# A mixer's output projection between the last steps of its recurrence, with reordered scaled products and a halved inverse level

## The reference, cut to what matters

```python
def wkv_scan(S0, r, w, k, v, kk, bb, reverse):
    def step(S, inp):
        rt, wt, kt, vt, kkt, bt = inp
        sk = jnp.einsum('bhij,bhj->bhi', S, kkt)
        S = S * wt[:, :, None, :] - sk[..., None] * bt[:, :, None, :] + vt[..., None] * kt[:, :, None, :]
        return S, jnp.einsum('bhij,bhj->bhi', S, rt)
    ...
# even_mixer, behind the two scans of each direction
o_lat = rwkv_output(ys_l[0] + ys_l[1], r_l, (dirs_l[0][1], dirs_l[1][1]), v_l, g_l, r_k, gn_w, gn_b)
out_lat = jnp.concatenate([o_lat, f_lat], axis=-1) @ w_out        # [256, 1024] @ [1024, 1024]
# the block, behind the mixer
h_lat = h_lat + m_lat[5] * o_lat
h_lat = half_ffn(h_lat, m_lat, 6, norm_g[i, 2], ffn2_w_gu[i], ffn2_w_down[i])   # rmsnorm, gate, up, silu, down
```

## Time and profile before

| | |
|---|---|
| median of three runs | 3303.49 us |
| the profiled execution | 3305.29 us |
| its span, first to last instruction | 3303.5 us |
| PE busy | 3195.9 us (97%), 28282 instructions |
| DVE busy | 2169.4 us (66%), 4656 instructions |
| ACT busy | 542.0 us (16%), 1073 instructions |
| GpSimd busy | 172.2 us (5%), 200 instructions |
| mean granted clock of PE | 0.989 |

### The profile page before, as it was taken

How to read it: one execution, slowest core, us unless ns; L and a number is a source line. 1 busy time by engine, 2 the same in 40 slices (tenths; PEclk the granted TensorE clock), 3 DMA queues, 4 the chain that set the end, 5 groups by cost and what they waited for, 6 DMA issues and landing times.

```text
span 3303.5 us, 64967 instructions
## 1 busy us (share of the span) xinstructions
PE 3195.9 (97%) x28282; PEld 2874.2 (87%) x28282; DVE 2169.4 (66%) x4656; ACT 542.0 (16%) x1073; POOL 172.2 (5%) x200
## 2 busy tenths in 40 slices
PE   7999999899999899999999999999999999999998
PEld 4888445588888799999889999999999999999998
DVE  6886347666676377676647657676667576776675
ACT  2000010234433110110121011122110102120111
POOL 1000000122222000000000000000000000000000
PEclk9999999999999899999999999999999999999999
DMA  7455555100000144444334465333444443334343
GB/s 287 178 220 220 223 211 221 44 6 6 7 6 7 51 160 173 154 171 174 131 129 171 173 209 183 117 127 136 162 158 175 147 160 116 128 122 166 136 171 115
DMA packets 69230, 466.48 MB, mean 141 GB/s; under 512 B 7296, under 2 KB 9984, under 8 KB 16217
## 3 DMA queue, kind: packets, MB, share of 16 engines
q1 hardware_dynamic: 51696, 368.07, 31.2%
q0 software_dynamic: 12192, 87.04, 7.0%
q10 hardware_dynamic: 5065, 7.27, 0.7%
HBM read 456.59 MB, written 5.77 MB: 140 GB/s over the span
## 4 chain that ended last, share of the span: by engine, by line
PE 91%; DVE 6%; ACT 2%; issue 1%; DMA 0%; POOL 0%; ACTq 0%; DVEq 0%; POOLq 0%
PE ps L776 31%; PE ps L1229 18%; PE ps L831 8%; PE ps L671 8%; PE ps L1380 4%; PE ps L855 4%; PE ps L906 1%; PE ps L893 1%; PE ps L912 1%; PE ps L1248 1%; PE ps L1303 1%; PE ps L1174 1%; PE ps L1278 1%; PE ps L953 1%; PE ps L1006 1%; PE ps L1355 1%
## 5 line engine op out<-in xcount | busy, mean ns | idle before, releaser
L776 PE MATMUL ps<-arena 128*128 128x128 f32 x4400 | 519.1, 275 | 0.0
L776 PEld LDWEIGHTS ps<-arena 128*128 128x128 f32 x4400 | 505.0, 192 | 0.0
L776 PE MATMUL ps<-arena,ring 128*128 128x128 f32 x2200 | 275.0, 275 | 0.0
L1825 DVE TENSOR_TENSOR arena<-arena,ps 128x256 f32<-128x256 f32 x146 | 61.5, 421 | 311.2 <-ACT arena L1431 285.3
L776 PEld LDWEIGHTS ps<-arena,ring 128*128 128x128 f32 x2200 | 260.9, 192 | 0.5
L1950 DVE CUSTOM_DVE_ANT_0 arena<-arena,vec 128x1024 f32<-128x1024 f32 x168 | 206.6, 1280 | 1.7 <-DMA arena<-in_ada_t 1.7
L1229 PE MATMUL ps<-y,arena 128*128 128x128 f32 x1584 | 193.3, 276 | 0.6 <-DVE y L2439 0.6
L1229 PEld LDWEIGHTS ps<-y,arena 128*128 128x128 f32 x1584 | 184.6, 192 | 4.8 <-issue 3.4
L1790 DVE TENSOR_TENSOR arena<-ring 128x512 f32<-128x512 f32 (+1 forms) x170 | 113.9, 670 | 60.0 <-DMA ring<-in_w_f_down 32.5
L671 PE MATMUL ps<-arena,ring 128*128 128x512 f32 x352 | 152.2, 592 | 0.0
L671 PEld LDWEIGHTS ps<-arena,ring 128*128 128x128 f32 x352 | 66.9, 190 | 83.8 <-issue 83.7
(11 more groups left out here) (393 smaller groups left out, 5871.5 us busy)
## 6 DMA issues: line engine op xcount, KB each, us to landing
ring<-in_w_f_gu SPq DMA_DIRECT2D x88, 1024.0 KB, 4.8
arena<-in_ada_t POOLq DMA_DIRECT2D x72, 1024.0 KB, 5.2
ring<-in_w_fx_gu SPq DMA_DIRECT2D x44, 1024.0 KB, 4.8
ring<-in_w_f_down SPq DMA_DIRECT2D x36, 1024.0 KB, 4.8
ring<-in_w_fx_down SPq DMA_DIRECT2D x24, 1024.0 KB, 4.8
ring<-in_w_qk_a SPq DMA_DIRECT2D x18, 1024.0 KB, 4.8
ring<-in_w_qk_r SPq DMA_DIRECT2D x16, 1024.0 KB, 4.8
ring<-in_w_v_r SPq DMA_DIRECT2D x16, 1024.0 KB, 4.8
```

The source lines that it names most:

```text
L776: last = mm(out, weights[number][:, j * P:(j + 1) * P], inputs[number](base + j), start=(s.opens and j == 0 and number in (1, 5)), stop=(s ...
```

## The change

The projection's weights are cut by input tile instead of output tile (`rows` in place of `cols`; `EVEN_ORDER` puts the two Fourier tiles first). Its 64 products run input tile by input tile into eight accumulating output tiles in banks 0, 1, 3 and 4: 40 of them behind the steps of period 12, 16 behind steps 1, 3 and 6 of period 13, and 8, those of tile 5, at the end. DVE takes each pair of output tiles out as it is complete; the norm's sums move to bank 5 and stand behind all products. Of the first two weight sums of `f2_0`, one moves to the end of period 12 and one behind the last update. In `scaled`, `bt` and `kt_` come before `kr`, PE waits for each by itself, `key_of` of an even unit moves from step 8 to step 5, and the operation L2196 moves from `key_scales` into `key_of`. Of level 5 only the half of `tri` that `halves_x` reads is computed; its transpose stays whole.

```diff
 STREAM += _ffn("f1_0", "ffn1_w_gu", DFF, "ffn1_w_down", 0)
-STREAM += [("e_in", 11, 1, "cols", "e_w_in", 0, 0), ("e_out", 4, 1, "cols", "e_w_out", 0, 0)]
+STREAM += [("e_in", 11, 1, "cols", "e_w_in", 0, 0), ("e_out", 4, 1, "rows", "e_w_out", 0, 0)]
+EVEN_ORDER = (6, 7, 0, 1, 2, 3, 4, 5)
 STREAM += _seven("f2_0", "ffn2_w_gu", DFF, "ffn2_w_down", 0) + _seven("f1_1", "ffn1_w_gu", DFF, "ffn1_w_down", 1)
...
+        def even_tile(m):
+            return ps[:, (0, 1, 3, 4)[m // 2], m % 2 * SEQ:(m % 2 + 1) * SEQ]
+        def norm_bank(name):
+            return 5 if name == "n2" else 4
         def norm_sums(t):
...
                     for k in range(tiles * g, tiles * g + tiles):
-                        last = mm(seg2(4)[:, 0:segs], ones[:], sq[:, :, k], start=(k == 0), stop=(k == KD - 1))
+                        last = mm(seg2(norm_bank(name))[:, 0:segs], ones[:], sq[:, :, k], start=(k == 0), stop=(k == KD - 1))
                     if g == groups - 1:
...
                     for c in range(4):
-                        for rows in (FIRST, SECOND):
+                        for rows in (sides(u)[:1] if lev == LEVELS - 1 else (FIRST, SECOND)):
                             last = mm(ps[rows, 0, at(hd, c)], tri_t[rows, q, hd, c], x_sb[rows, hd, c],
...
             def keys_tok(u):
-                pe.wait_ge(*past(f"dve.kt{u}"))
+                pe.wait_ge(*past(f"dve.bt{u}"))
                 if u % 2 == 0:
...
                     pe.wait_ge(*past(f"dve.bon_v{u // 2}"))
+                pe.wait_ge(*past(f"dve.kt{u}"))
                 for c in range(4):
...
                 pe.wait_ge(*past(f"act.g{u // 2}"))
+                pe.wait_ge(*past(f"dve.kr{u}"))
                 if u % 2:
...
+            even_slots, even_made = list(slots_flat("e_out")), [0]
+            def even_products(count):
+                for i in range(even_made[0], even_made[0] + count):
+                    n, m = divmod(i, KD)
+                    k, s = EVEN_ORDER[n], even_slots[n // 2]
+                    if i == 0:
+                        pe.wait_ge(*past(f"act.x{UNITS - 1}_{LEVELS}"))
+                        pe.wait_ge(*past(f"dve.t_off{UNITS - 1}"))
+                        pe.wait_ge(*past(f"dve.k_mix{UNITS - 1}"))
+                    if i % 16 == 0:
+                        pe.wait_ge(landed[s.pos], landed_by("e_out", s))
+                    if m == 0 and k < KR:
+                        pe.wait_ge(*past(f"dve.mixed{k}"))
+                    w = ring[:, s.pos, (n % 2 * KD + m) * P:(n % 2 * KD + m + 1) * P]
+                    last = mm(even_tile(m), w, y1(k), start=(n == 0 and m % 2 == 0), stop=(n == KD - 1), skip_group_check=True)
+                    if i % 16 == 15:
+                        last.then_inc(slots_used, 1)
+                    elif n == KD - 1 and m % 2:
+                        last.then_inc(*step(f"pe.even{m // 2}"))
+                even_made[0] += count
+            BESIDE_CHUNKS = (0, 0, 4, 4, 4, 4, 4, 4, 4, 3, 3, 3, 3)
+            BESIDE_READOUT = {1: 3, 3: 3, 6: 10}
+            def beside(p, n):
+                if p == UNITS:
+                    even_products(BESIDE_CHUNKS[n])
+                elif p == UNITS + 1:
+                    even_products(BESIDE_READOUT.get(n, 0))
             for p in range(-1, UNITS + 2):
...
                     between(p, 2 * lev - 1)
+                    beside(p, 2 * lev - 1)
                     if unit(p):
...
                     between(p, 2 * lev)
+                    beside(p, 2 * lev)
                 if unit(p):
...
                 between(p, 2 * LEVELS - 1)
+                beside(p, 2 * LEVELS - 1)
                 if unit(p):
...
                 between(p, 2 * LEVELS)
-            pe.wait_ge(*past(f"dve.mixed{KR - 1}"))
-            linear("e_out", y1, SEQ, behind=sums_behind("n2"))
+                beside(p, 2 * LEVELS)
+            even_products(KD)
+            norm_sums_of = sums_behind("n2")
+            for g in range(4):
+                norm_sums_of(g)
             seven("f2_0", y1, "n2", sums_behind("n3"))
...
                 act.wait_ge(*past(f"pe.{name}_sum"))
-                f(rs[:, 0:segs], seg2(4)[:, 0:segs], ACT.Sqrt, bias=V("eps6"), scale=1.0 / D) \
+                f(rs[:, 0:segs], seg2(norm_bank(name))[:, 0:segs], ACT.Sqrt, bias=V("eps6"), scale=1.0 / D) \
                     .then_inc(*step(f"act.{name}_std"))
...
-            def first_weight_sums(name):
-                for s, stage in seven_slots(name)[0:2]:
+            def first_weight_sums(name, which=slice(0, 2)):
+                for s, stage in seven_slots(name)[which]:
                     weight_sums(s, stage)
...
                         continue
-                    if s.item == 3:
+                    if s.item == 3 and name != "e_out":
                         first_weight_sums(after_third)
-                    v.wait_ge(slots_used, s.n + 1)
+                    if name == "e_out" and s.item < 3:
+                        v.wait_ge(*past(f"pe.even{s.item}"))
+                    else:
+                        v.wait_ge(slots_used, s.n + 1)
                     for m in range(tiles):
...
                             assert segs == 1
-                            last = stt(hv, tile_of(s, m),
+                            last = stt(hv, even_tile(k) if name == "e_out" else tile_of(s, m),
                                        gate_f[:, bass.ds(at + 2 * k + sgm, 1)], hv, ALU.mult, ALU.add)
                     last.then_inc(psum_free, 1)
+                    if s.item == 3 and name == "e_out":
+                        first_weight_sums(after_third, slice(1, 2))
...
                 v.wait_ge(*past(f"pe.t{u}_{lev}"))
-                tt(eight(tri[:, q]), eight(tri[:, q]), four_eight(0), ALU.subtract).then_inc(*step(f"dve.t{u}_{lev}"))
+                rows = sides(u)[0] if lev == LEVELS - 1 else slice(0, P)
+                tt(eight(tri[rows, q]), eight(tri[rows, q]), four_eight(0)[rows], ALU.subtract) \
+                    .then_inc(*step(f"dve.t{u}_{lev}"))
                 v.wait_ge(*past(f"pe.tt{u}_{lev}"))
...
                     v.wait_ge(*past(f"pe.k_mix{u - 1}"))
-                ts(kd, rate[:, d], V("k_a", t), omka[:, t:t + 1], ALU.mult, ALU.add).then_inc(*step(f"dve.kd_a{u}"))
                 tt(bb, kk, rate[:, d], ALU.mult).then_inc(*step(f"dve.bb{u}"))
...
                 d, t = u % 2, u // 2
+                v.wait_ge(*past(f"act.sig{t}"))
+                ts(kd, rate[:, d], V("k_a", t), omka[:, t:t + 1], ALU.mult, ALU.add).then_inc(*step(f"dve.kd_a{u}"))
                 v.wait_ge(*past(f"dve.kd_a{u}"))
...
                 v.wait_ge(*past(f"act.exp{u}"))
+                v.wait_ge(*past(f"dve.bb{u}"))
+                tt(bt, bb, p_inv_f, ALU.mult).then_inc(*step(f"dve.bt{u}"))
+                tt(kt_, kd, p_inv_f, ALU.mult).then_inc(*step(f"dve.kt{u}"))
                 tt(kr[:, g, 0:4], kk.rearrange("p (c t) -> p c t", c=4), ex, ALU.mult)
-                tt(kr[:, g, 4:6], r_of(u // 2).rearrange("p (c t) -> p c t", c=2), own[:, 0:2], ALU.mult)
-                tt(bt, bb, p_inv_f, ALU.mult)
-                tt(kt_, kd, p_inv_f, ALU.mult).then_inc(*step(f"dve.kt{u}"))
+                tt(kr[:, g, 4:6], r_of(u // 2).rearrange("p (c t) -> p c t", c=2), own[:, 0:2], ALU.mult) \
+                    .then_inc(*step(f"dve.kr{u}"))
                 for j in range(3):
...
                         key_inverse(u // 2, n)
+                    elif n == 5:
+                        key_of(u)
                     elif n == 7:
...
                     elif n == 8:
-                        key_of(u)
                         scaled(u)
...
                 fill(p, 12)
+                if p == UNITS:
+                    first_weight_sums("f2_0", slice(0, 1))
             v.wait_ge(*past(f"dve.mixed{KR - 1}"))
...
             laid = laid[list(E_IN_PAIRS)] if name == "e_in" else laid
+        elif cut == "rows":
+            laid = w[list(EVEN_ORDER)].reshape(n_slots, 2, P, KD, P).transpose(0, 2, 1, 3, 4)
         elif cut == "pair":
```

More of the change, by code:

```diff
@@ L86 @@
            "w_in_2", "w_attn_proj_2", "w_ret_proj_2", "w_out_2", "w_ffn_gate_2", "w_ffn_up_2", "w_ffn_down_2")
-SLOT_USED = {"cols": SLOT, "pair": SLOT, "down": DOWN_SLOT, "tall": SLOT, "flat": 3 * 512, "quarters": SLOT, "quarters_cols": SLOT,
+SLOT_USED = {"cols": SLOT, "rows": SLOT, "pair": SLOT, "down": DOWN_SLOT, "tall": SLOT, "flat": 3 * 512, "quarters": SLOT, "quarters_cols": SLOT,
              "quarters_tall": SLOT, "quarters_pairs": SLOT,
```

## The result

The changed kernel takes 3271.69 us (median of four runs, 3270.77 to 3272.80) against 3304.68 us (four runs, 3298.15 to 3306.09): 33.0 us less, a ratio of 0.9901 with a 95% interval of 0.9887 to 0.9915. I had forecast 3283.7 us, 3276 to 3293: right in direction, 13 us short in size, outside my range. The profiled execution took 3271.81 us with a span of 3270.0 us, 33.5 us less than the one before.

What follows compares the result with a forecast made beforehand. TensorE was taken as the bound (91% of the chain of waits). Terms 15.6 (tail) - 0.6 (halved level) + 3.1 (scaled products) + 1.7 (clock) = 19.8 us took the median from 3303.5 to 3283.7 us, range 3276 to 3293.

Steps and rivals of the forecast that it cites:

- Part 1, waits: Output projection between the steps of periods 12 and 13: its products cover PE's waits there, 10.2 us gained.
- the 6.8 us of the clock: Low clock from 1098.5 to 1119.1 us: gapless PE brings the full clock, saving half of 13.6 busy us.
- The rival in which the clock stays low: Tail: clock is low when the products begin and stays low, so 6.8 us don't come; 3290.5 us, chance 13%.
- Part 1, switching: Tail: changing between kinds of product costs 0.1 us for each of 14 groups, 1.4 us lost; bounds 0 to 2.4.
- Part 2: Last inverse level (5) on half: halved instructions on one array quarter save no time; 0.6 us lost over 12 units.
- Part 3: Scaled products reordered: transposes' 1.58 us wait goes, about 1.06 us comes at level 4 in even units; net 3.1 us gained.
- The clock in the recurrence: Unit 0's first product comes sooner, 1.3 us; one of two low stretches behind transposes' waits goes, 1.7 us.
- The rival in which the new wait brings the clock down: Level 4 of even units: the new 1.06 us wait lowers the clock, slower than before; 3307.5 us, chance 3%.
- Behind the mixer: Everything after the first idle product behind period 13: no gain forecast, 0 us.

Runs made afterwards that it cites:

- one_block: Changed kernel with period 12's 40 projection products in one block at its end instead of behind eleven steps: 3284.55 us, ratio 0.9942.
- key_at_6: Changed kernel with key_of of even units at step 6, behind level 3's update, instead of step 5: 3269.33 us, ratio 0.9896.
- early: mixed_best with four projection products put into period 11's last two waits, 36 instead of 40 left in period 12: 3264.05 us, ratio 0.9875.
- full_level: Changed kernel with level 5 computed on both halves again: 3270.05 us, ratio 0.9907.
- order_only: Changed kernel with the key's operations back at step 8 (odd units: L2196 back in key_scales), new order of scaled products kept: 3269.39 us, ratio 0.9897.
- unit0_busy: Kernel before with nine idle products in unit 0 in front of the transposes, nothing else changed: 3303.70 us, ratio 0.9999.
- tail_only: Kernel before with only the projection moved between the steps and the weight sums split: 3281.14 us, ratio 0.9940.
- keys_back: Changed kernel with the order and place of the scaled products as before: 3283.49 us, ratio 0.9947.
- filler: Kernel before with idle products in the waits of periods 12 and 13, projection still at the end, nothing moved: 3294.55 us, ratio 0.9969.
- no_tail: Changed kernel with the projection behind period 13 again; halved level and reordered scaled products kept: 3294.06 us, ratio 0.9976.
- mixed_best: Changed kernel with key_of of even units at step 6 and odd units' key scale back in key_scales: 3267.00 us, ratio 0.9882.
- place_only: Changed kernel with the old order inside scaled, PE waiting for both, key's operations still at step 5: 3277.16 us, run once.

## Why the prediction was right or wrong

**Part 1, waits: right.** All three waits of period 13, the nine of period 12 and the last one went, 10.2 us, and the 6.8 us of the clock came. The rival in which the clock stays low didn't happen in any of the nine profiles whose products cover every step of period 12.

**Part 1, switching: the step that failed.** I charged 1.4 us for 14 changes between kinds of product, from one row of a 256-column pair. Its successor works on quarters of the array (64*64); the steps' products, like the projection's, use all of it (128*128). There the rows show almost nothing: the six instructions at 1106.00 take 1.30 us to their successor, 0.43 a pair as in a row, and the eight at 1085.45 take 1.78 (to 1087.23), 0.05 us more than four pairs in a row. So the term was wrong in itself, and one was missing. Measured is 3.0 us on the other side (20.0 - 10.2 - 6.8), 4.4 us off, 0.23 us for each of the 13 waits that went. The wait in brackets begins where the last matmul has run out. What a wait costs is more, 0.27 us by the rows of L988: 0.66 us for its four instructions until PE is called idle, 0.39 us when a long product follows. Of that, 0.11 us is what a wait adds to the row's own length (0.66 against 0.55): its first weight load begins together with it there (both at 1081.98 in one_block), and 0.21 us ahead of it without a wait. The rest is the run-out. The runs agree in size, not to the hundredth: 0.26 us a wait in one_block, 1.80 us gained for a wait of 1.58 in key_at_6, 1.4 for two waits of 1.23 in early. My bounds, 0 to 2.4 us lost, excluded a gain for no reason.

**Part 2: right that it gives nothing, 0.6 us off.** One quarter of the array takes as long for 16 instructions as two for 32; full_level and the changed kernel have the same intervals. The Trainium skill (TensorEngine Tiling (Array Packing), Key Properties) says that the array's tiles work independently and in parallel; the rows agree: 32 instructions over two tiles take 0.98 us, 16 on one 0.97.

**Part 3: mechanism right, sizes small.** The wait at the transposes went and a wait of 0.90 us came at the place named, where I had computed 1.06. The wait that went was worth more than its 1.58 us: from the last chunk step in front of the transposes to L915 behind them (L992 to L906 before) it takes 1.37 us instead of 3.15. The new wait costs 0.96 (from L997, L988 before, to L902: 1.38 us instead of 0.42). So an even interval gained 0.83 and not 0.52 us: 1.5 us more in five. Odd ones lost 0.11 each but for the first, as computed. That the move is a loss by itself I computed in its parts (1.06 us against what the order alone would do), but I didn't draw the conclusion; order_only and key_at_6 show it.

**The clock in the recurrence: the second step that failed.** I gave 1.3 us for unit 0 and 1.7 for one of two low stretches behind the transposes' waits. In unit 0 the strict product came 1.3 us sooner, right, but the low stretch behind it also went, 2.2 us (unit0_busy shows it by itself). A second one of 3.4 us, behind a wait of 1.56 us for L902 in the next interval, stayed; it is in seven of the eight profiles with the new order and costs 0.6 us (29.38 us against 28.79 without it, in early). Of the others both went, 3.1 us. The profiles say how regular this is: the kernels with the wait of 1.58 us (before, tail_only, keys_back, unit0_busy, filler) have 8 low stretches in 25 even intervals, those with the new order (after, no_tail, full_level, order_only, key_at_6, one_block, mixed_best, early) none in 40, and neither has place_only, with waits of 0.90 and 0.65 us, in 5. The rival in which the new wait brings the clock down is out: 25 such waits of 0.90 us stand in profiles with it (after, full_level, one_block, no_tail, place_only), and no low stretch follows one.

**Behind the mixer** I had 0 and the profiles differ by 3.1 us, nearly all by one low stretch in o_out. Whether the change has a part in it is open (four of four profiles with the old tail have one there, four of ten with the new). The sum of the misses is 4.4 + 0.6 + 1.5 + 0.1 + 2.2 + 1.4 + 0.4 (before unit 0) + 3.1 = 13.7 us, what lies between 33.5 and 19.8.

On the scatter: runs of before spread over 14 us, the four of the changed kernel over 2 (the five of key_at_6 over 10). My range took the old scatter for the new one, and centred it on one profile.

## What to carry to other kernels

A wait of TensorE costs more than the idle time in its row: in small-product code add the run-out and the next weight load (here 0.1 to 0.3 us), and ask whether a low clock follows it. Work that doesn't depend on the chain belongs into such waits in pieces a little longer than they are; even idle products there gained 8 us in their stretch here, and the kernel with them is 11 us faster. Halving instructions that alternate over two quarters of the array gives nothing when those left all fall on one. And when operations are moved ahead of a wait, look at what stands behind the new place: one step later was 1 us an even unit better.

## What the runs showed of the hardware

- The clock's low stretches make most of this kernel's scatter. The fastest run of the kernel before (3294.5 us) has a mean granted clock of 0.993, the slowest (3308.3 us) one of 0.988: 0.005 of 3300 us is 16 us of full-speed work, an estimate and an upper bound for the 13.8 us between them. In the tail low stretches covered 27 us in one profile and 41 in another, with the same instructions there; in the ten profiles with all of period 12's waits filled, by products or by idle ones, there was at most one of some 6.9 us, at its start.
- A low stretch can hold with PE busy 31 of 41 us (unit0_busy's last row) and a low stretch begins behind waits of 1.6 us in some places of the same code and not in others (two of five in the kernel before).
